# Depthwise convolution over four shifted copies of 32 channels, norm sums by channel chunk, and attention heads in pairs

## The reference, cut to what matters

```python
# layer 0: neighbourhood attention, 8 heads of 64; 256 local keys (masked) and 256 context keys
s_loc = einsum(q_r, k_nb) * scale + bias          # bias: relative position, gathered
s_ctx = einsum(q_r, k_ctx) * scale
p = softmax(concat([s_loc, s_ctx]))
out = p_loc @ v_nb + p_ctx @ v_ctx
# layer 1: Conformer convolution module, 31 taps, 1024 channels
a, g = split(h @ pw1_w + pw1_b, 2)
u = a * sigmoid(g)
u = depthwise_conv(u, dw_w) + dw_b                # each channel by itself, zero padding 15 on both sides
u = silu(layer_norm(u, ln_g, ln_b))               # over the 1024 channels of a token
y = u @ pw2_w + pw2_b
```

## Time and profile before

| | |
|---|---|
| median of 3 runs (lowest to highest) | 1152.77 us (1150.54 to 1154.02) |
| the profiled execution: time / span | 1153.78 us / 1151.9 us |
| PE, PEld, DVE, ACT, POOL busy | 90%, 72%, 69%, 58%, 5% |
| mean granted clock of PE | 0.942 |
| prelude, to the first input projection | 0 to 46 us |
| input projections of layer 0 | 46 to 173.5 us |
| attention | 173.5 to 234.3 us |
| output projection, routing and experts of layer 0 | to 615 us |
| norm, pw1, convolution | 615 to 733.1 us |
| layer norm of the convolution, silu, pw2 | to 774 us |
| routing and experts of layer 1, final norm | to 1151.9 us |

### The profile page before, as it was taken

How to read it: one execution, slowest core, us unless ns; L and a number is a source line. 1 busy time by engine, 2 the same in 40 slices (tenths; PEclk the granted TensorE clock), 3 DMA queues, 4 the chain that set the end, 5 groups by cost and what they waited for, 6 DMA issues and landing times.

```text
span 1151.9 us, 16779 instructions
## 1 busy us (share of the span) xinstructions
PE 1035.3 (90%) x5876; PEld 832.2 (72%) x5876; DVE 798.2 (69%) x1051; ACT 667.1 (58%) x882; POOL 52.3 (5%) x85
## 2 busy tenths in 40 slices
PE   3899999986699999999994999785699999999995
PEld 0478775582588888888883999673588888888883
DVE  0631344333599898998967689544598998997993
ACT  2522317612388877878764656321577877876672
POOL 3630000000000000000000000000000000000000
PEclk9899999997699999999996999896699999999998
DMA  9987997725799899998993321001599899997870
GB/s 358 278 274 240 361 357 254 241 83 192 264 360 368 311 354 345 342 370 309 352 335 104 118 74 37 1 1 68 200 352 360 310 368 330 351 355 260 294 255 38
DMA packets 137432, 294.38 MB, mean 256 GB/s; under 512 B 11343, under 2 KB 40159, under 8 KB 137368
## 3 DMA queue, kind: packets, MB, share of 16 engines
q1 hardware_dynamic: 132288, 284.20, 69.4%
q0 software_dynamic: 3536, 8.52, 2.5%
q10 hardware_dynamic: 1544, 0.83, 0.3%
HBM read 292.39 MB, written 1.12 MB: 255 GB/s over the span
## 4 chain that ended last, share of the span: by engine, by line
PE 83%; DVE 9%; DMA 3%; ACT 2%; issue 1%; ACTq 0%; DVEq 0%
PE ps L1546 15%; PE ps L1548 14%; PE ps L1547 14%; PE ps L2008 4%; PE ps L1557 4%; PE ps L1790 3%; PE ps L1646 3%; DMA raw<-in_w_mod 3%; DVE wlo L1273 2%; PE ps L1647 2%; PE ps L1648 2%; PE ps L1664 1%; PE ps L1705 1%; PE ps L1736 1%; PE ps L1666 1%
## 5 line engine op out<-in xcount | busy, mean ns | idle before, releaser
L1273 DVE TENSOR_TENSOR wlo<-raw,whi 128x1024 fp32r<-128x1024 f32 x384 | 454.8, 1223 | 43.8 <-ACT whi L670 37.4
L670 ACT CAST whi<-raw 128x1024 fp32r<-128x1024 f32 x384 | 398.0, 1054 | 94.9 <-PE ps L1548 94.2
L1546 PE MATMUL ps<-whi,xghi 128*128 128x512 f32 x480 | 193.2, 403 | 13.8 <-DVE xglo L1279 13.8
L1548 PE MATMUL ps<-wlo,xghi 128*128 128x512 f32 x480 | 189.6, 395 | 0.0
L1547 PE MATMUL ps<-whi,xglo 128*128 128x512 f32 x480 | 188.2, 392 | 0.0
L972 DVE TENSOR_TENSOR wlo<-raw,whi 128x1024 fp32r<-128x1024 f32 x56 | 70.4, 1274 | 70.9 <-ACT whi L665 70.9
L1546 PEld LDWEIGHTS ps<-whi,xghi 128*128 128x128 f32 x480 | 91.3, 190 | 32.2 <-issue 13.7
L1548 PEld LDWEIGHTS ps<-wlo,xghi 128*128 128x128 f32 x480 | 91.1, 190 | 21.4
L1547 PEld LDWEIGHTS ps<-whi,xglo 128*128 128x128 f32 x480 | 91.3, 190 | 19.4
L1546 PE MATMUL ps<-whi,hidThi 128*128 128x512 f32 x256 | 101.6, 397 | 1.4 <-issue 1.4
L1548 PE MATMUL ps<-wlo,hidThi 128*128 128x512 f32 x256 | 100.5, 392 | 0.0
(11 more groups left out here) (312 smaller groups left out, 1600.5 us busy)
## 6 DMA issues: line engine op xcount, KB each, us to landing
raw<-in_moe_w SPq DMA_DIRECT2D x384, 512.0 KB, 5.2
raw<-in_w_mod SPq DMA_DIRECT2D x96, 512.0 KB, 6.4
raw<-in_na_w_in SPq DMA_DIRECT2D x24, 512.0 KB, 6.6
raw<-in_cf_pw_w SPq DMA_DIRECT2D x24, 512.0 KB, 4.6
mods<-mod_scratch POOLq DMA_DIRECT2D x9, 512.0 KB, 5.0
raw<-in_ab_w_out SPq DMA_DIRECT2D x8, 512.0 KB, 5.8
bias<-bias_scratch POOLq DMA_DIRECT2D x32, 64.0 KB, 6.3
ctxt<-in_ctx SPq DMA_DIRECT2D x1, 1024.0 KB, 10.3
```

The costliest lines, as they stand in the source:

```text
L670: A.copy(whi[:, (MOE_W[tn.L] + j) % SPL, :], raw[:, (MOE_U[tn.L] + j) % RAW, :]).then_inc(tn.sem("w_rounded"), 1)
L1273: V.tensor_tensor(wlo[:, n % SPL, :], raw[:, (MOE_U[L] + j) % RAW, :], whi[:, n % SPL, :], ALU.subtract).then_inc(tn.sem("unit_done"), 1)
L1546: T.matmul(dst, lhi, rhi, start=first, stop=False)
L1548: return T.matmul(dst, lhi, rlo, start=False, stop=last)
```

## The change

The convolution is formed by PE alone. SP copies each finished chunk of `uT` within SBUF into `urep`: for each of the four groups of 32 channels four copies, the copy on partitions 32s to 32s + 31 shifted by s tokens (16 transfers of 32 partitions by 284 floats for each chunk, 128 in all). A stationary tile of 128 rows by 32 columns (four stacked diagonals of taps 4j to 4j + 3) then does four taps of 32 channels; 8 steps by 4 column groups make a chunk, 32 matmuls. DVE builds the 32 tiles of a chunk in one instruction (`stack`); ACT adds the bias and squares (`conv_out`), and one matmul of 512 columns sums both over channels (`channel_sums`). The variance is mean square less squared mean. `dwst` is loaded with the taps in that order, by 5 transfers in runs of 32 floats. In the attention two heads of a pair alternate from step to step, DVE adds the bias in PSUM and scales by the reciprocal, and `attend` forms both heads of a pair with alternating halves of the columns. `bias_scratch` holds 64 copies of each row, and is written after the first 16 units. Places in the arena move.

```diff
-PE_TAPS = (13, 13, 13, 13, 13, 13, 20, 20)
-MAX_TAPS = max(PE_TAPS)
+SHIFTS = 4
+STEPS = (TAPS + SHIFTS - 1) // SHIFTS
+REP = SEQ + SHIFTS * (STEPS - 1)
+UPAD = SEQ + 32
...
-            load_dense(SECOND, SECOND_U)
+            def replicate(ch):
+                eng.wait_ge(gate_set, ch + 1)
+                if ch >= 3:
+                    eng.wait_ge(diag_used, ch - 2)
+                for s in range(SHIFTS):
+                    for g in range(SHIFTS):
+                        eng.dma_start(urep[s * QUAD:(s + 1) * QUAD, ch % 3, g, :],
+                                      uT[g * QUAD:(g + 1) * QUAD, ch, s:s + REP]).then_inc(rep_in[ch % 3], 16)
+            cuts = [0, 14, 18, 22, len(SECOND)]
+            for j in range(4):
+                load_dense(SECOND[cuts[j]:cuts[j + 1]], SECOND_U + cuts[j])
+                replicate(2 * j)
+                replicate(2 * j + 1)
...
-            eng.dma_start(bias_scratch, rpbt[:]).then_inc(rpb_out, 16)
+            eng.wait_ge(tensor_unit, 2 * KC)
+            eng.dma_start(bias_scratch, rpbt[:].unsqueeze(1).broadcast_to([HEADS * 7, GRID_W, P])).then_inc(rpb_out, 16)
...
-            eng.dma_start(dwst[:], cf_dw_w[0]).then_inc(rows_in, 16)
+            for s in range(SHIFTS + 1):
+                rows = slice(0, STEPS) if s < SHIFTS - 1 else slice(0, STEPS - 1) if s < SHIFTS else slice(STEPS - 1, STEPS)
+                first = s if s < SHIFTS else TAPS - 1
+                at_s = min(s, SHIFTS - 1) * QUAD
+                dst = dwst[rows, :].rearrange("j (g n) -> j g n", g=D // QUAD)[:, :, at_s:at_s + QUAD]
+                src = bass.AP(tensor=cf_dw_w.tensor, offset=first * D,
+                              ap=[[SHIFTS * D, rows.stop - rows.start], [QUAD, D // QUAD], [1, QUAD]])
+                eng.dma_start(dst, src).then_inc(rows_in, 16)
...
-                if n < 16:
-                    eng.wait_ge(recips, n + 1)
-                    A.activation(prob[:, n % 2, :], prob[:, n % 2, :], ACT.Copy, scale=smx[:, 2, n % 2:n % 2 + 1]).then_inc(normed, 1)
...
-            def diags(ch):
...
-                for tap in range(PE_TAPS[ch]):
-                    A.activation(dg[:, (ch % 2) * MAX_TAPS + tap, :], ident, ACT.Copy, scale=dwT[:, ch, tap:tap + 1]) \
-                     .then_inc(diag_set, 1)
+            def conv_out(ch):
+                eng.wait_ge(diag_used, ch + 1)
+                bias_of = cols[:, R_DWB + ch:R_DWB + ch + 1]
+                A.activation(cT[:, ch, :], ps[:, ch, 0:SEQ], ACT.Identity, bias=bias_of).then_inc(conv_set, 1)
+                A.activation(cs[:, ch, 1, :], ps[:, ch, 0:SEQ], ACT.Square, bias=bias_of).then_inc(conv_set, 1)
...
                 round_second(4 * (j + 1) + 6)
-                for m in range(2):
-                    diags(2 * j + m)
+                if j:
+                    conv_out(2 * j - 2)
+                    conv_out(2 * j - 1)
...
+                h, t = 2 * (n // 4) + n % 2, n // 2 % 2
                 eng.wait_ge(scores, n + 1)
+                eng.wait_ge(bias_masked, h + 1)
+                local = ps[:, 4 + n % 2, 0:SEQ]
+                link(V.tensor_tensor(local, local, bias[:, h, t, :], ALU.add))
                 V.tensor_reduce(smx[:, 0, n % 2:n % 2 + 1], ps[:, 4 + n % 2, :], AX.X, ALU.max, negate=True).then_inc(biased, 1)
...
+                link(V.reciprocal(smx[:, 2, n % 2:n % 2 + 1], smx[:, 1, n % 2:n % 2 + 1]))
+                V.tensor_scalar(prob[:, n % 2, :], prob[:, n % 2, :], smx[:, 2, n % 2:n % 2 + 1], None, ALU.mult).then_inc(normed, 1)
...
-            def conv(c0, until):
...
+            def stack(ch):
+                if ch >= 2:
+                    eng.wait_ge(diag_used, ch - 1)
+                full = [P, SHIFTS, STEPS, QUAD]
+                one = cst[:, C_STACK:C_STACK + QUAD].unsqueeze(1).unsqueeze(1).broadcast_to(full)
+                V.tensor_tensor(dg[:, ch % 2], one, wq[:, SHIFTS * ch:SHIFTS * (ch + 1), :].unsqueeze(3).broadcast_to(full), ALU.mult) \
+                 .then_inc(diag_set, 1)
...
-                conv(2 * j, 4 * (j + 1) + 6 if j < 3 else 18)
+                rest_second(4 * (j + 1) + 6 if j < 3 else len(SECOND) - 2)
+                stack(2 * j)
+                stack(2 * j + 1)
...
+            total, squared = ps[:, 0, 0:SEQ], ps[:, 0, SEQ:2 * SEQ]
+            link(V.tensor_scalar(mB[:], total, 1.0 / D, None, ALU.mult))
+            link(V.scalar_tensor_tensor(out=vB[:], in0=total, scalar=-1.0 / D, in1=mB[:], op0=ALU.mult, op1=ALU.mult))
+            link(V.scalar_tensor_tensor(out=vB[:], in0=squared, scalar=1.0 / D, in1=vB[:], op0=ALU.mult, op1=ALU.add))
+            V.tensor_scalar(vB[:], vB[:], 0.0, EPS, ALU.max, ALU.add).then_inc(centred, 1)
...
+            for g in range(D // QUAD):
+                ins = T.transpose(ps[:, 5, g * STEPS:(g + 1) * STEPS], dwst[:, g * P:(g + 1) * P], cst[0:STEPS, C_ID:C_ID + STEPS])
...
-                T.matmul(ps[:, 4 + n % 2, 0:SEQ], cst[:, C_FLIP:C_FLIP + P], bias[:, h, t, :],
-                         start=False, stop=True).then_inc(scores, 1)
...
+            def attend(n):
+                hp, t = n // 4, n // 2 % 2
+                eng.wait_ge(probT_set, n + 2)
+                if n % 4 == 0 and hp >= 2:
+                    eng.wait_ge(a_rest, hp - 1)
+                for q in range(4):
+                    for m in (n, n + 1):
+                        h, lo = 2 * hp + m % 2, m % 2 * DH
+                        ins = T.matmul(ps[lo:lo + DH, 2 + hp % 2, t * P:(t + 1) * P], vv[:, q, h * DH:(h + 1) * DH],
+                                       probT[:, m % 4, q, :], start=(q == 0), stop=(q == 3))
+                ins.then_inc(attended, 1)
...
             def conv(ch):
+                eng.wait_ge(rep_in[ch % 3], 16 * SHIFTS ** 2 * (ch // 3 + 1))
+                eng.wait_ge(diag_set, ch + 1)
+                for j in range(STEPS):
+                    for g in range(SHIFTS):
+                        ins = T.matmul(ps[g * QUAD:(g + 1) * QUAD, ch, 0:SEQ], dg[:, ch % 2, g, j, :],
+                                       urep[:, ch % 3, g, SHIFTS * j:SHIFTS * j + SEQ], start=(j == 0), stop=(j == STEPS - 1))
+                ins.then_inc(diag_used, 1)
...
             def channel_sums(ch):
+                eng.wait_ge(conv_set, 2 * ch + 2)
+                ins = T.matmul(ps[:, 0, :], ones[:], cs[:, ch].rearrange("p a n -> p (a n)"), start=(ch == 0), stop=(ch == KC - 1))
...
+                    channel_sums(2 * j - 3)
             conv(6)
+            channel_sums(4)
+            channel_sums(5)
             conv(7)
-            channel_sums(4)
             channel_sums(6)
...
+            channel_sums(7)
```

More of the change, by code:

```diff
@@ L395, in program @@
         exped = sem("exped")
-        recips = sem("recips")
         normed = sem("normed")
@@ L430, in program @@
         centred = sem("centred")
-        sq_set = sem("sq_set")
+        rep_in = [sem(f"rep_in{i}") for i in range(3)]
         s_act = sem("s_act")
@@ L935, in _ @@
                 round_second(4 * (j + 1) + 6)
[L936 to L937 removed]
+                if j:
+                    conv_out(2 * j - 2)
+                    conv_out(2 * j - 1)
             round_second(len(SECOND) - 2)
[L940 to L946 removed]
+            conv_out(6)
+            conv_out(7)
+            A.activation(stat[:, 2, 2:3], stat[:, 0, 0:1], ACT.Sqrt)
+            eng.wait_ge(centred, 1)
+            A.activation(rB[:], vB[:], ACT.Sqrt).then_inc(root, 1)
+            A.activation(stat[:, 2, 3:4], stat[:, 0, 0:1], ACT.Silu)
+            for q in range(4):
+                eng.wait_ge(centred, 2 + q)
                 for ch in (2 * q, 2 * q + 1):
@@ L1726, in _ @@
                 mods_before(FIRST.index(("mod", 10, 0)), 1 + n % 2)
-                if n:
-                    m = n - 1
-                    h, t = m // 2, m % 2
-                    eng.wait_ge(probT_set, m + 1)
-                    hp, lo = h // 2, (h % 2) * DH
-                    if m % 4 == 0 and hp >= 2:
-                        eng.wait_ge(a_rest, hp - 1)
-                    for q in range(4):
-                        ins = T.matmul(ps[lo:lo + DH, 2 + hp % 2, t * P:(t + 1) * P], vv[:, q, h * DH:(h + 1) * DH],
-                                       probT[:, m % 2, q, :], start=(q == 0), stop=(q == 3))
-                    ins.then_inc(attended, 1)
+                if n and n % 2 == 0:
+                    attend(n - 2)
             eng.wait_ge(a_rest, 4)
@@ L2039, in _ @@
                     channel_sums(2 * j - 4)
+                    channel_sums(2 * j - 3)
             conv(6)
+            channel_sums(4)
+            channel_sums(5)
             conv(7)
-            channel_sums(4)
             channel_sums(6)
-            for k in range(KC):
-                if k % 2 == 0:
-                    eng.wait_ge(sq_set, k // 2 + 1)
-                ins = T.matmul(ps[:, 1, 0:SEQ], ones[:], sq[:, k, :], start=(k == 0), stop=(k == KC - 1))
-            ins.then_inc(ln_sum, 1)
+            channel_sums(7)
             npj = 0
```

137 lines of the change are left out of this document (44 added, 93 removed).

## The result

The changed kernel takes 1171.05 us (median of 4 runs, 1169.41 to 1171.79) against 1151.82 for the kernel before (4 runs): ratio 1.016, 95% interval 1.0137 to 1.0182. It is slower by 19 us, where 20 less were forecast. Its profiled execution has a span of 1169.3 us, 17.4 above that of before. Among all executions of this document one, of d1_attention, took 1521.47 us at a granted clock of 0.645; it is left out of the comparisons.

What follows compares the result with a forecast made beforehand. PE was taken to bound attention and convolution, weight loads and PE's transposes the prelude. Terms 16.9 + 3.6 + 9.8 - 0.3 - 10 = 20.0 us took 1153.78 to 1133.8 profiled, 1132.8 as median; range 1119 to 1143.

Steps and rivals of the forecast that it cites:

- the price of a copy's issue: Convolution: SP issues 32 transfers for each j at 0.40 us, 12.8 us, against 21.5 of PE.
- the third rival: Convolution: the copies bound it, eating the 20.0 us and 3.5 more from 0.80 us an issue; chance 0.05.
- that rival's own formula: Convolution: at p us an issue, conv(7) is late by 32p - 14.3 and each of three rounds by 32p - 21.5.
- the sum: Whole kernel: 16.9 + 3.6 + 9.8 - 0.3 - 10 = 20.0 us less.
- a prelude that doesn't move: Prelude, first rival: the long runs held ACT, so the loss doesn't come and the time is 1122.8 us; chance 0.20.
- Convolution, gain 16.9: Convolution with channel sums: 102.4 us become 85.95 and a 0.4 us wait goes; gain 16.9, from 14 to 19.
- Copies: Convolution: copies stay hidden; the last has 4.0 us to land, 1.5 of slack if it takes the estimated 2.5.
- Norm, gain 3.6: Norm behind the convolution: 10.1 us from the last sum to the reciprocal's end become 6.5.
- Attention, gain 9.8: Attention: two steps go from 7.84 to 5.8 us; the output projection starts at 224.5 against 234.26 us.
- Prelude, loss 10: Prelude: 993 more packets on ACT's queue hold rb; ACT starts at 32.2 us and the transposes start 10 later.
- Transposes of the taps, 0.3: Ahead of the first projection: 24 more transposes, 3.6 us, mostly fall into PE's wait; loss 0.3.
- the bias write, nothing: POOL: the 1.8 MB write sets its loads back some 25 us; no cost unless its traffic starves PE's units.

Runs made afterwards that it cites:

- d1_attention: The kernel before with the change's attention alone; prelude, constants, arena and convolution as before: 1145.28 us, 0.9926 of the kernel before.
- b1_arena: The kernel before with 160 unused bytes ahead of the arena, all work unchanged: 1165.60 us, 1.0109 of the kernel before.
- a1_arena: The changed kernel with 352 unused bytes ahead of the arena, restoring its address in the kernel before: 1162.51 us.
- c1_all_three: The changed kernel with 352 bytes ahead of the arena, taps' loads on POOL and half the copies on POOL: 1120.94 us, 0.9732 of the kernel before.
- a3_two_queues: The changed kernel with eight of each chunk's sixteen copies issued by POOL, the other eight by SP: 1146.53 us, 0.9954 of the kernel before.
- c4_wide: The changed kernel with four copies of 128 partitions a chunk, not sixteen; same bytes, part of the convolution left out: 1146.05 us, one execution.
- a2_taps_pool: The changed kernel with the five loads of the taps issued on POOL's queue and not on ACT's: 1160.66 us.
- e1_front64: d4_place128 with raw, whi, wlo and all other tiles ahead of the arena 64 bytes higher, the arena unmoved: 1124.08 us, one execution.
- e2_both64: d4_place128 with the tiles ahead of the arena and the arena itself both 64 bytes higher: 1120.81 us, one execution.
- d2_xghi: c1_all_three with the tile xghi alone moved, to the residue of the slow arena: 1127.17 us, one execution.
- d4_place128: c1_all_three with 416 bytes ahead of the arena in place of 352, at the residue of whi: 1121.72 us, one execution.

## Why the prediction was wrong

**The step that failed first is the price of a copy's issue**, "SP issues 32 transfers for each j at 0.40 (0.80 for two)". The row behind it is of weight loads in another stage. The copies took 0.67 on the average. The nearest row, since it is of many small transfers in a row, was POOL's at 0.64, and it was used only as the weak end of the third rival. At 0.67 that rival's own formula gives 7 us for conv(7) and nothing for the rounds. The copies cost 24.5 by the medians and 27.5 by the stage, for two terms that the formula left out. The list of SP also holds two to four weight loads a round (1.1 to 2.2 us), so a round of the queue takes 23.2 to 24.2 us (649.38, 672.93, 697.15, 720.34) against PE's 21.2 (12.0 of pw1, 7.3 of convolution, 1.9 of sums), and what is late isn't made good in any round: 20.6 us of waits. And four of the five waits took the clock with them, 7.1 more. The third rival was the right one: at 0.67, and not from 0.80 on, the copies cost more than the 20.0 of the sum. 0.05 was too little for it.

**The second is a term that was missing**: that shrinking `cst` and widening `wq` moves every tile behind them. It is 11.2 us by the stages (1.6 of the projections' 2.9, and 5.4 and 4.2 in the experts), 13.6 by b1_arena, 8.5 by the medians of a1_arena and 13 by its profiled execution. The sum took every stage that the edits don't touch as unchanged.

Between the forecast of 20.0 less and the 17.4 more of the two spans lie 37.4 us. The convolution is 27.1 of them and the place 11.2; what is left of all other terms is -0.9, in which the 2.5 us that the two routings give back cover 1.3 lost in the projections and 0.9 in the attention. c1_all_three, with copies, taps and place mended, took 1120.94; the prediction's terms give 1122.8 for a prelude that doesn't move. That this agrees within 2 us is in part luck, since small errors of both signs cancel. No kernel with the copies and the place mended and the taps left was run.

Term by term:
- Convolution, gain 16.9: right where the copies don't bind (85.2 in a3_two_queues against 102.4, 17.2). A chunk took 3.66 for the 3.8 assumed, two sums 1.91 for 1.90. The quarters do work side by side, with four stationary tiles: 32 matmuls in 3.66 us, where one full one took 0.43.
- Copies: they land in 1.9 us, for which 2.5 was assumed. The Trainium skill (DMA: Bandwidth & Descriptors, Rules for kernel authors) wants small transfers coalesced. For the reason of latency, which the prediction weighed, it didn't matter. It did for the issue: in c4_wide SP's issue costs the same for 4 times the bytes. Whether fewer copies can make the four shifts wasn't tried.
- Norm, gain 3.6: 6.3 us from the last sum to the reciprocal's end, for 6.5; gain 3.8.
- Attention, gain 9.8: 8.9 in the changed kernel. A pair of steps takes 5.87 (207.12 to 212.99 in its chain) for 5.8, and 16 records of products of the 64-column halves take 1.02, where 8 took 1.01: they overlap. The term lost 0.9 at the start, where a first gap and the lower clock after it weren't foreseen: at a clock of 1.00 (a1_arena) it is 9.3, at 0.64 (d1_attention) 5.7.
- Prelude, loss 10: 9.9, and ACT's first square at 32.19. a2_taps_pool gives it back. That nothing later gives any of it back was not quite so: the routing gave 2.1. Of the mechanism (a queue that must drain before the next issue) the runs show that the taps' loads hold the issues behind them, in either layout. That it is the count of packets isn't shown, and the 9.9 for the forecast 10 may be luck: the 31-row load held them for 9.45 us with few packets. By the Trainium skill (DMA: Bandwidth & Descriptors, "Why a DMA increments its semaphore by 16 and not by 1") 31 rows go through one engine. No row here shows single engines, and ACT wasn't free sooner with the rows in eights, as the prediction thought possible, but 10 us later.
- Transposes of the taps, 0.3, and the bias write, nothing: the projections lost 2.9, of which 31 units at 0.05 of place are 1.6; what is left, about 1.3, agrees with the 1.6 of d1_attention.

## What to carry to other kernels

Price an issue by a row of the same kind of transfer in a run of many, add everything else in that queue's list, and compare its round with PE's: a queue is an engine with its own pitch, and when its round is the longer one, halving the list brought the whole gain back, and so did a quarter of the count (in c4_wide, which leaves out the shifts). When a stage that nothing touched gets slower at full clock and without gaps, look at what moved in SBUF before looking at the work: an unused pad in the kernel before is a run of its own, and it would have shown 13 us here. A cost in another stage is best told apart by reading the same events in both chains.

## What the runs showed of the hardware

- How fast PE's matmuls follow each other depends on how far the arena's tiles lie from `whi` and `wlo`, modulo 256 bytes: a turn of four experts, back to back at a granted clock of 1.00, takes 72.60, 73.17, 74.25, 74.38 or 74.60 us at distances of 0, -64, -128, -96 and +96 bytes, and moving both tiles together changes nothing (e1_front64, e2_both64). With the roles exchanged (the projections) -64 is best, and 0 is as slow as the others: 2.14 against 2.19 us a unit. Why is open, and so is which two accesses meet, since in d2_xghi the matmuls on a tile that hadn't moved got slower too. Other distances weren't tried.
- SP needs 0.59 us (median) for a copy from SBUF to SBUF, whether it has 32 partitions or 128, and 0.66 to 0.68 on the average of 32 in a row; POOL needs 0.498.
- Behind a load of 31 rows of 4 KB the second next issue took ACT 9.45 us. Five loads of 1024 pieces of 128 bytes in all took 11.37 for themselves and 1.24 and 7.98 for the two behind them. Without them `rw` and `rb` go out in 0.41 and 0.77 us.
- After a gap of PE of 2.65 to 2.66 us at the start of the attention the granted clock over 17.7 us (from 4.6 ahead of the gap's end) was 0.63 to 0.65 in three profiled executions, 0.71 in three, 0.81 in eight and 1.00 in two (a1_arena, d4_place128), all of the same instructions there. In the convolution of the changed kernel waits of 5.56, 3.52, 6.88 and 2.58 us were followed by some us at 0.50, one of 2.05 wasn't.
